# Cross-attention of an encoder step: rounded three-product values and another order of scores, turns and the last mean

## The reference, cut to what matters

```python
def _mem_attn(h, mk, mv, w_q, q_norm, w_o):
    q = _rmsnorm((h @ w_q).reshape(bsz, t, X_HEADS, X_HEAD_DIM), q_norm)
    logits = einsum("bthd,bmhd->bhtm", q, mk) * (X_HEAD_DIM ** -0.5)
    probs = softmax(logits, axis=-1)
    o = einsum("bhtm,bmhd->bthd", probs, mv).reshape(bsz, t, X_HEADS * X_HEAD_DIM)
    return o @ w_o
```

## Time and profile before

| what | value |
|---|---|
| median of 3 runs | 1736.86 us |
| profiled execution, its own time | 1742.67 us |
| its span on the core | 1740.9 us |
| mean granted TensorE clock | 0.971 |
| TensorE matmul busy | 1651.5 us, 95% |
| VectorE busy | 1037.2 us, 60% |
| ScalarE busy | 629.0 us, 36% |
| GpSimd busy | 594.1 us, 34% |
| DMA | 153.47 MB, 88 GB/s |

### The profile page before, as it was taken

How to read it: one execution, slowest core, us unless ns; L and a number is a source line. 1 busy time by engine, 2 the same in 40 slices (tenths; PEclk the granted TensorE clock), 3 DMA queues, 4 the chain that set the end, 5 groups by cost and what they waited for, 6 DMA issues and landing times.

```text
span 1740.9 us, 30533 instructions
## 1 busy us (share of the span) xinstructions
PE 1651.5 (95%) x11888; PEld 1553.4 (89%) x11890; DVE 1037.2 (60%) x1322; ACT 629.0 (36%) x913; POOL 594.1 (34%) x239
## 2 busy tenths in 40 slices
PE   5999888899899999999999989899999999999999
PEld 5959863599699999999999989799789999999999
DVE  5678997356535556456655879755635555036630
ACT  4332226333533333133333564333534333123320
POOL 2314411033023334334333433633113434433432
PEclk9969998899999999999999999999999999999999
DMA  4322331024022222222222222324112222222232
GB/s 169 111 85 97 100 109 37 13 85 170 25 72 85 84 85 96 75 84 84 89 100 81 95 97 73 121 88 144 72 37 73 85 86 101 79 80 89 84 100 86
DMA packets 41712, 153.47 MB, mean 88 GB/s; under 512 B 5344, under 2 KB 5856, under 8 KB 40360
## 3 DMA queue, kind: packets, MB, share of 16 engines
q1 hardware_dynamic: 41640, 152.46, 26.3%
HBM read 145.22 MB, written 9.32 MB: 89 GB/s over the span
## 4 chain that ended last, share of the span: by engine, by line
issue 51%; PE 27%; POOL 11%; DVE 8%; ACT 1%; DMA 1%; POOLq 0%; SPq 0%; DVEq 0%; ACTq 0%
PE PS L808 25%; POOL WLO L398 11%; DVE SC L1281 1%; PE AX L908 1%; DVE M L1280 1%; DVE SQA L1193 1%; DVE YC L1331 1%; DVE YC L1336 0%; DVE WLO L1345 0%; POOLq L424 0%; DVE CB L1316 0%; DVE CB L1181 0%; DMA WRAW<-in_w_mv 0%; DMA X<-in_x 0%; DVE AST L1326 0%
## 5 line engine op out<-in xcount | busy, mean ns | idle before, releaser
L398 POOL TENSOR_TENSOR WLO<-WRAW,WHI 128x1024 fp32r<-128x1024 f32 (+2 forms) x231 | 593.5, 2570 | 1102.1 <-ACT WHI L438 1101.9
L438 ACT ACTIVATE WHI<-WRAW 128x1024 fp32r<-128x1024 f32 (+1 forms) x237 | 262.6, 1108 | 716.0 <-PE PS L808 662.2
L808 PE MATMUL PS<-XH,WHI 128*128 128x274 f32 x2256 | 481.3, 295 | 34.9 <-POOL WLO L398 26.3
L808 PE MATMUL PS<-XH,WLO 128*128 128x274 f32 x2256 | 477.2, 293 | 0.0
L808 PE MATMUL PS<-XL,WHI 128*128 128x274 f32 x2256 | 474.7, 292 | 0.0
L808 PEld LDWEIGHTS PS<-XH,WHI 128*128 128x128 f32 x2256 | 363.3, 192 | 41.0 <-POOL WLO L398 26.3
L808 PEld LDWEIGHTS PS<-XL,WHI 128*128 128x128 f32 x2256 | 362.0, 192 | 0.0
L808 PEld LDWEIGHTS PS<-XH,WLO 128*128 128x128 f32 x2256 | 361.5, 192 | 0.0
L808 PE MATMUL PS<-HH,WHI 128*128 128x274 f32 x1216 | 257.2, 293 | 0.7 <-DVE HL L1385 0.7
L808 PE MATMUL PS<-HH,WLO 128*128 128x274 f32 x1216 | 254.6, 291 | 0.0
L808 PE MATMUL PS<-HL,WHI 128*128 128x274 f32 x1216 | 254.4, 291 | 0.0
(11 more groups left out here) (233 smaller groups left out, 1700.7 us busy)
## 6 DMA issues: line engine op xcount, KB each, us to landing
WRAW<-in_w_in_even SPq DMA_DIRECT2D x29, 512.0 KB, 3.8
WRAW<-in_w_up0a SPq DMA_DIRECT2D x22, 512.0 KB, 3.6
WRAW<-in_w_up0b SPq DMA_DIRECT2D x22, 512.0 KB, 3.6
WRAW<-in_w_up1a SPq DMA_DIRECT2D x22, 512.0 KB, 3.6
WRAW<-in_w_up1b SPq DMA_DIRECT2D x22, 512.0 KB, 3.7
WRAW<-in_w_mv SPq DMA_DIRECT2D x16, 512.0 KB, 3.7
WRAW<-in_w_xq SPq DMA_DIRECT2D x16, 512.0 KB, 3.6
WRAW<-in_w_xo SPq DMA_DIRECT2D x16, 512.0 KB, 3.7
```

The source lines that it names most:

```text
L398: pool.tensor_tensor(WLO[parity][:, 0:cols], WRAW[parity][:, 0:cols], WHIf[parity][:, 0:cols], ALU.subtract).then_inc(lo_done, 1)
L438: act.activation(WHI[parity][:, 0:cols], WRAW[parity][:, 0:cols], ACT.Copy).then_inc(hi_done, 1)
L808: ins = pe.matmul(dst, w, x, start=first, stop=last)
```

## The change

Seven edits:

- The turned probabilities are split: ScalarE copies them rounded into PTH, and VectorE subtracts for the rest, PTL (`turn_low`, semaphore xt_low). The sample unit keeps the plain PTX.
- The memory values are split as well: ScalarE rounds MV into MVH while it is in head 1 of the projection, VectorE writes MVL = MV − MVH in head 2. MVL lies where MV lay, so VectorE first waits until the stores of the memory outputs have landed.
- `values(s)` of a prompt unit becomes three fp32r products in place of one float32 product.
- TensorE's order becomes scores(1), head_mean(3), scores(2), turn(0), values(0), turn(1), scores(3), values(1), turn(2), scores(4), values(2), turn(3), values(3), turn(4), values(4). Scores(1) waits for the eviction of chunk 6 and scores(2) for that of chunk 7.
- VectorE's order becomes, for s = 2 to 7, maximum(s), normalise(s−1), turn_low(s−2), low_part(s−3). Head 3's `query_head` stands right after maximum(1), and head 2's before the last eviction of the projection.
- ScalarE takes the root of head 3 directly after its square, before exponentials(1).
- SP stores MK and MV before it issues the query weights, and no longer after the caches.

The core of the diff:

```diff
-        PTX = at("PTX", [P, 2, 2, 512], F32, XHL_AT)
+        PTH, PTL = pack(XHL_AT, HHL_AT, [("PTH", [P, 2, 2, 512], F32R), ("PTL", [P, 2, 2, 512], F32R)])
+        PTX = at("PTX", [P, 256], F32, XHL_AT + 16384)
+        MVH = at("MVH", [P, 2, D], F32R, S2 + 8 * T * 4)
+        MVL = at("MVL", [P, 2, D], F32R, M_AT + 8192)
...
@@ SP
-                stream(f"xq{l}")
-                sp.wait_ge(*((yl_even, A_TILES + 5) if l == 0 else (chunk_done, C0["out_odd"])))
-                sp.dma_start(CK[:], a["cache_mk"][l]).then_inc(cache_landed, 16)
-                sp.dma_start(CV[:], a["cache_mv"][l]).then_inc(cache_landed, 16)
                 sp.wait_ge(*((hn_out, HN0["mk0"] + 4) if l == 0 else (k1_out, 2)))
                 n += store(o["mem_k"][l], MK[:])
                 sp.wait_ge(evicted, T0[f"mv{l}"] + 2)
                 n += store(o["mem_v"][l], MV[:])
+                stream(f"xq{l}")
+                sp.wait_ge(*((yl_even, A_TILES + 5) if l == 0 else (chunk_done, C0["out_odd"])))
+                sp.dma_start(CK[:], a["cache_mk"][l]).then_inc(cache_landed, 16)
+                sp.dma_start(CV[:], a["cache_mv"][l]).then_inc(cache_landed, 16)
@@ ScalarE, in cross(l)
+                    if hd == 1:
+                        act.wait_ge(evicted, T0[f"mv{l}"] + 2)
+                        for mb in range(2):
+                            act.activation(MVH[:, mb, :], MV[:, mb, :], ACT.Copy).then_inc(mvh_ready, 1)
                     if hd == 2:
                         exponentials(0)
                     if hd < XHEADS - 1:
                         ahead(c0 + 2 * hd + 2)
                         head_std(u0 + hd, False)
+                head_std(u0 + XHEADS - 1, False)
                 for s in range(1, 7):
...
-                            act.activation(PTX[:, v % 2, :, :], AX[:, 0:2, :], ACT.Copy).then_inc(xt_read, 1)
+                            act.activation(PTH[:, v % 2, :, :], AX[:, 0:2, :], ACT.Copy).then_inc(xt_read, 1)
...
-                    if s == 1:
-                        head_std(u0 + XHEADS - 1, False)
@@ TensorE, in cross(l)
-                    if s == 1:
-                        pe.wait_ge(evicted, t0 + 8)
+                    if s in (1, 2):
+                        pe.wait_ge(evicted, t0 + 6 + s)
...
                     if s:
                         pe.wait_ge(xt_read, b + s)
-                    if s < 2:
-                        pe.wait_ge(hn_std, u0 + 3 + s)
+                        pe.wait_ge(xt_low, low_turns(l, s))
+                    else:
+                        pe.wait_ge(hn_std, u0 + XHEADS)
...
                     if u < 4:
+                        pe.wait_ge(mvl_ready, 2 * l + 2)
+                        pe.wait_ge(xt_low, low_turns(l, s + 1))
                         for d in range(2):
+                            w = slice(P * (2 * u + d), P * (2 * u + d) + P)
                             for mb in range(2):
-                                ins = pe.matmul(AX[:, 2 + d, :], MV[:, mb, P * (2 * u + d):P * (2 * u + d) + P],
-                                                PTX[:, s % 2, mb, :], start=mb == 0, stop=mb == 1)
+                                ins = product([AX[:, 2 + d, :]], MVH[:, mb, w], MVL[:, mb, w], [PTH[:, s % 2, mb, :]],
+                                              [PTL[:, s % 2, mb, :]], mb == 0, mb == 1)
...
                 scores(1)
+                head_mean(u0 + XHEADS - 1)
+                scores(2)
                 turn(0)
-                scores(2)
-                pe.wait_ge(xt_read, b + 1)
-                head_mean(u0 + 3)
                 values(0)
                 turn(1)
-                for s in range(3, 5):
-                    scores(s)
-                    turn(s - 1)
-                    values(s - 2)
+                scores(3)
+                values(1)
+                turn(2)
+                scores(4)
+                values(2)
+                turn(3)
+                values(3)
                 turn(4)
-                values(3)
                 values(4)
@@ VectorE, in cross(l)
+                def values_low(mb):
+                    dve.wait_ge(mvh_ready, 2 * l + mb + 1)
+                    dve.wait_ge(out_stored, 16 * (8, 13)[l])
+                    dve.tensor_tensor(MVL[:, mb, :], MV[:, mb, :], MVH[:].bitcast(F32)[:, mb, :], ALU.subtract).then_inc(mvl_ready, 1)
+
+                def turn_low(s):
+                    if XUNITS[s] < 4:
+                        dve.wait_ge(xt_read, b + s + 1)
+                        if s >= 2:
+                            dve.wait_ge(xpv_done, b + s - 1)
+                        dve.tensor_tensor(PTL[:, s % 2, :, :], AX[:, 0:2, :], PTHf[:, s % 2, :, :], ALU.subtract).then_inc(xt_low, 1)
+
                 for hd in range(XHEADS):
                     evict(c0 + 2 * hd, t0 + 2 * hd, (t0 + 2 * hd) % 2, QX[:, 2 * hd, :])
                     if hd == 3:
                         normalise(0)
-                    elif hd:
+                    if hd:
                         query_head(hd - 1)
                     evict(c0 + 2 * hd + 1, t0 + 2 * hd + 1, (t0 + 1) % 2, QX[:, 2 * hd + 1, :])
-                    if hd == 3:
-                        query_head(2)
                     head_sum(u0 + hd, T)
                     if hd == 2:
                         maximum(0)
+                        for mb in range(2):
+                            values_low(mb)
                 maximum(1)
+                query_head(XHEADS - 1)
                 for s in range(2, 8):
+                    if s < 5:
+                        maximum(s)
                     if s < 6:
                         normalise(s - 1)
+                    if s < 7:
+                        turn_low(s - 2)
                     if s >= 3:
                         low_part(s - 3)
-                    if s < 5:
-                        maximum(s)
-                    if s == 2:
-                        query_head(XHEADS - 1)
```

More of the change, by code:

```diff
@@ L210, in build @@
         PX0, PX1 = at("PX0", [P, 4, MEM], F32, HTAIL), at("PX1", [P, 4, MEM], F32, LTAIL)
-        PTX = at("PTX", [P, 2, 2, 512], F32, XHL_AT)
+        PTH, PTL = pack(XHL_AT, HHL_AT, [("PTH", [P, 2, 2, 512], F32R), ("PTL", [P, 2, 2, 512], F32R)])
+        PTHf = PTH[:].bitcast(F32)
+        PTX = at("PTX", [P, 256], F32, XHL_AT + 16384)
+        MVH = at("MVH", [P, 2, D], F32R, S2 + 8 * T * 4)
+        MVL = at("MVL", [P, 2, D], F32R, M_AT + 8192)
+        assert S2 + 8 * T * 4 + 8192 <= END
         GB, YB, GE, H32 = pack(S2, END, [("GB", [P, 552], F32), ("YB", [P, T], F32), ("GE", [P, T], F32),
@@ L263, in build @@
         xt_read, xpv_done, xyh, xyl = sem("xt_read"), sem("xpv_done"), sem("xyh"), sem("xyl")
+        mvh_ready, mvl_ready, xt_low = sem("mvh_ready"), sem("mvl_ready"), sem("xt_low")
         gb_ready, gconv0, gconv, gelu_done = sem("gb_ready"), sem("gconv0"), sem("gconv"), sem("gelu_done")
@@ L287, in build, with low_turns @@
         LEN = {p[0]: p[1] for p in PHASES}
+        assert T0["xq0"] % 2 == T0["xq1"] % 2 == 1
+        def low_turns(l, s):
+            return 4 * l + sum(u < 4 for u in XUNITS[0:s])
         def odd_key_mean(p):
@@ L362, in _ @@
                     n += store(o["h_last"], HST[:])
+                sp.wait_ge(*((hn_out, HN0["mk0"] + 4) if l == 0 else (k1_out, 2)))
+                n += store(o["mem_k"][l], MK[:])
+                sp.wait_ge(evicted, T0[f"mv{l}"] + 2)
+                n += store(o["mem_v"][l], MV[:])
                 stream(f"xq{l}")
@@ L368, in _ @@
                 sp.dma_start(CV[:], a["cache_mv"][l]).then_inc(cache_landed, 16)
[L369 to L372, removed]
                 stream(f"xo{l}")
@@ L645, in cross @@
                         if XUNITS[v] < 4:
-                            act.activation(PTX[:, v % 2, :, :], AX[:, 0:2, :], ACT.Copy).then_inc(xt_read, 1)
+                            act.activation(PTH[:, v % 2, :, :], AX[:, 0:2, :], ACT.Copy).then_inc(xt_read, 1)
                         else:
-                            act.activation(PTX[:, v % 2, 0, 0:256], AX[:, 0, 0:256], ACT.Copy).then_inc(xt_read, 1)
-                    if s == 1:
-                        head_std(u0 + XHEADS - 1, False)
+                            act.activation(PTX[:], AX[:, 0, 0:256], ACT.Copy).then_inc(xt_read, 1)
                     if s >= 2:
@@ L1066, in values @@
                                 ins = pe.matmul(AX[:, 2, 32 * m:32 * m + 32], CV[:, mb, P * m:P * m + P],
-                                                PTX[:, s % 2, 0, at_:at_ + 32], start=mb == 0, stop=mb == 1)
+                                                PTX[:, at_:at_ + 32], start=mb == 0, stop=mb == 1)
                     ins.then_inc(xpv_done, 1)
```

## The result

The changed kernel takes 1783.4 us (median of 4 runs, 1778.58 to 1784.76), against 1738.11 us of the kernel before on the same chip (median of 4 runs, 1736.64 to 1744.08): ratio 1.0249, 95% interval 1.0217 to 1.0281. The forecast was 1773, range 1750 to 1785, slower with 0.91. So sign, mechanism and the stated range hold, and the size came out at +45 where +36 was forecast. The median lies near the range's upper end and 0.4 us above the 1762 to 1783 that the forecast mechanism had for itself.

What follows compares the result with a forecast made beforehand. The prediction took the wait ending last, not any engine's busy share, as the bound, with the change putting rounds in series through VectorE. 17.0 us at full clock plus 19.2 for the clock, 36.2 on 1736.86, made 1773; range 1750 to 1785.

Steps and rivals of the forecast that it cites:

- Hidden parts: MVH copies, MVL subtractions and moved memory stores beside the query projection: cost 0, stores bounded by −1 and +4 us.
- The start: From scores(1) to values(0): VectorE's queue lets values(0) go at 454.75, 3.3 us late, with TensorE idle 6.0 us.
- The loop: Rounds with maximum first on VectorE: all in series, 12.6 us a unit, idle 5.3 us or so before each values.
- The tail: Values(3) to the output projection: two waits of 2.8 us; projection at 495.85 against 488.14, +7.7 us in layer 0.
- Cheaper values: Prompt units' values as twelve rounded matmuls: 2.8 us a step against 3.43, eight steps giving back 5.2 us.
- Full-clock sum: Both cross-attention stages at full clock throughout: 56.4 us each, +7.7 and +9.3, together +17.0 us.
- The clock: TensorE at half clock behind waits: 2.2 us for each of three long waits, 3 for the tail, 19.2 us in all.
- (a): Rival: the same steps, but waits too short to lose the clock; +17, 1754 us; chance 0.15.
- (b): Rival: clock low nearly everywhere, bursts of 7 us broken by waits of 5.4; 32 and 17, 1786 us; chance 0.10.
- (c): Rival: faster, VectorE's part of a round finishes under TensorE's scores and turn, waits vanish; 1725 us; chance 0.07.
- (d): Rival: waits shorter by half through some misread order, and the clock stays; about 1740 to 1750 us; chance 0.08.

Runs made afterwards that it cites:

- e8: Kernel before with only the memory stores moved and, in each layer, the two MVH copies and two subtractions beside the query projection; 1738.7 us, ratio 0.9993.
- e4: Changed kernel with unread matmuls (18, 18, 18, 9, 9) in front of the five values steps; 1756.9 us, ratio 1.0101 to the kernel before.
- e7: Changed kernel with turn(4) moved in front of values(3) and nothing else; 1769.7 us, ratio 1.0175 to the kernel before.
- e5: Changed kernel with the maximum last in VectorE's round and turn(4) in front of values(3); 1740.2 us, ratio 1.0000 to the kernel before.
- e6: Changed kernel without its split, maximum last in VectorE's round, turn(4) in front of values(3); 1736.0 us, ratio 0.9992 to the kernel before.
- e1: Changed kernel with one edit, the maximum last in VectorE's round; 1752.5 us, ratio 1.0072 to the kernel before.
- e2: Changed kernel without its split (plain float32 values), all its orders kept; 1765.6 us, ratio 1.0145 to the kernel before.
- e11: Kernel before with 3, 3 and 4 unread matmuls in the tail of each layer; 1735.7 us, ratio 0.9977.
- e9: Changed kernel without split, maximum last, turn(4) before values(3), and 3, 3 and 4 unread matmuls in the tail; 1730.6 us, ratio 0.9940 to the kernel before.

## Why the prediction was right, point by point

- **Hidden parts.** Right: e8, and the idle times left. The bound of +4 us for the stores was not needed.
- **The start.** Right to 0.1 us. Values(0) was forecast 15.35 us behind the start of scores(1) and came at 447.90 − 432.46 = 15.44. The head sum took 1.10 us where I took 1.0. One step off this path was too short: scores(2) was to end 8.4 us behind the start, 4.1 behind the last mean's start, and turn(0) started at 8.9; so the wait was 5.52 and not 6.0 us, and nothing came later by it.
- **The loop.** Right: three long waits of 5.52, 5.15, 5.15 us, where 6.0 and 5.3 stood; a round of 12.6 us at full clock (e4). A reading of today's loop was wrong: the last mean does not lie between values(0) and values(1) but ahead of values(0), at 450.44. Between them lies this wait, the longest of the old stage, which I had left out with my "0.65 to 1.32 us":

```profile
457.66 3.61 PE L1032 MATMUL PS<-CK,QX 128*32 128x256 f32 x16 [1.71 <-issue]
```

- **The tail.** The waits were 2.74 and 2.75 where 2.8 stood. The mechanism is shown by e7.
- **Cheaper values.** Right: 2.85 us a step in e4 (448.50 to the turn at 451.35), where 2.8 was forecast and 3.43 stood.
- **Full-clock sum.** 17.0 forecast; 19.9 by e4, whose layer 0 still had 3.4 us of low clock (a turn of 1.95 us and part of the sample's step). Its layer 1, at 1.00 throughout, took 57.2 us where the chain had 56.4; twice that would make 18.6.
- **The clock.** This term was mis-sized in its two parts, though its sum came near: 19.2 forecast; 19.5 as the difference to e4; 22.6 against the full-clock chain, summed over the steps below, and with that 17.0 + 22.6 = 39.6 us where 39.4 was measured. A values step behind a long wait lost 1.4 to 2.4 us (4.25 to 5.20 us in place of 2.8), 10.6 us over six waits where 6 × 2.2 = 13.2 stood. The tail lost more: 14.9 and 16.4 us from values(3) to the projection, where 9.65 is the full-clock chain, so 5.3 and 6.7 against 3 each; layer 1 lies just outside the bound of 6.5. I had reasoned that two waits of 2.8 us would lose little; there the clock was at 0.50 for 13.7 and 17.1 us on end. The sum for today's tail, "3.0 + 0.95 + 3.4 = 7.4", was right by luck: the turn of 0.95 lies ahead of 475.89, and a wait of 1.02 us that I had left out stands in its place.
- **Rivals.** (a), the clock holds, would give 1754; e4, which forces it, gives 1756.9. (b) is the tail, not the rounds. (c) fell: its condition, VectorE's part finishing under scores and turn, is what e5 and e6 restore, and even there the time is 1740 and 1736 us and not 1725. (d) fell with the length of the waits.
- **What stays open.** Stages and medians do not agree fully: the stages of the profiled executions differ by 39.4 us, the medians by 45.3. The profiled executions themselves differ by 35.9 us, 1778.58 less 1742.67; that this is nearly the 36.2 of the sum is chance, since the stages gave 39.4 and the rest of the span gave 3.9 back that was not forecast. Outside the two stages the thirteen profiled executions spend 1638.6 to 1645.7 us, with no relation to the edits that I can see; the low-clock intervals there differ in length from run to run, 85 us in all in before's execution and 72 in after's. Executions without a trace differ in the same way: the four of after have spans of 1776.4 to 1782.6 us at mean clocks of 0.962 to 0.959, and the 25 of before beside e5 to e8 go from 1733.1 us at 0.975 to 1743.9 at 0.970. So the spread of one kernel goes mostly with the clock. Where in those executions the time at half clock lies isn't recorded, so the 6 us between stages and medians stay open.

In the kernel that the Trainium skill describes ("TensorE: Matmul & The Clock Gate", "HAM oscillation — how this bites in real kernels"), whose bursts of matmuls are separated by waits for DMA, every burst starts at the lower clock. The traces here agree for the waits of 4.19 to 5.52 us of after and e1, and not throughout for shorter ones: behind the waits of 4.06 us in e2 the burst started at half clock in layer 0 and at full in layer 1, and behind the same wait of 2.74 us the sample's step started at full clock in layer 0 of after and at half in layer 1. Of the rounds they add that the clock came back inside each burst, 2.9 to 5.1 us into it.

## What to carry to other kernels

In an engine that runs in a written order, put the step whose input comes last at the end of a round, behind the steps that others wait for: one maximum in front made four steps of VectorE and the matmuls serial, and moving it gave back 31 us of 45. Write out the chain between two starts of the same step, not the busy shares; VectorE was 41% busy in the stage (27.2 of 66.3 us) and set its length. And price a wait of TensorE above its length: in the changed kernel 42.6 us of waits for VectorE had another 19.5 us of clock loss beside them, and matmuls that nobody reads won those back.

## What was not expected of the hardware

Adding work made kernels faster: 72 unread matmuls a layer in e4 took 26.5 us off, ten took 0.23% off the kernel that stood before. And short waits cost clock in one place and not in another: behind the waits of 0.72, 0.65 and 1.02 us in the tail of the kernel before the clock was at half for 10.2 and 6.8 us, while in the rounds of e6, with waits up to 1.11 us, and in those of the kernel before, with waits of 1.32 and 1.71, it stayed at 1.00. Layer 1 of e11 and layer 0 of e9 show that the tail can be kept at 1.00; what makes the two differ was not tried. One rival to the waits stands in the traces: the clock fell inside the sample's step, TensorE's run of 32-column matmuls, in layer 0 of before (0.5 us into it), of after (2.0) and of e4 (3.1), in e4 behind waits of 1.39 us and less. Whether that step loses the clock by itself, or only with short waits beside it, no run here parts.
